# Mixer projection begins with index and latent columns; its other four groups become units beside preparing, turning and index; modulation spread 13, 13, 10 over three stages

## The reference

```python
(q_a, k_a, v_a, f_a, q_b, k_b, v_b, q_c, c_kv, q_i, k_i, w_i, gates) = jnp.split(h @ w_in, _split_points(), axis=-1)
y_a = forgetting_attention(heads(q_a, 6), heads(k_a, 6), heads(v_a, 6), f_a + b_forget)   # cumulated log sigmoid(f) as bias
y_b = stick_breaking_attention(heads(q_b, 5), heads(k_b, 5), heads(v_b, 5))
k_c, v_c = jnp.split(rmsnorm(c_kv, g_kv) @ w_kv_up, 2, axis=-1)
q_c, k_c, q_i = partial_rope of each;  k_i = partial_rope(rmsnorm(k_i, g_idx_k))
y_c = dsa_attention(q_c, k_c, v_c, q_i, k_i, w_i)   # keys: the top 64 of an index score relu(q_i k_i) w_i
merged = g_a*(y_a @ w_up_fox) + g_b*(y_b @ w_up_sb) + g_c*(y_c @ w_up_dsa);  return merged @ w_out
```

## Time and profile before

| | us |
|---|---|
| Median of 3 runs (2890.78 to 2898.58) | 2893.74 |
| The profiled execution | 2897.77 |
| Its span, first to last instruction | 2896.0 |
| PE busy | 2670.3 (92%) |
| DVE busy | 1427.1 (49%) |
| ACT busy | 1188.7 (41%) |
| Mean granted TensorE clock, as share of full | 0.946 |

### The profile page before, as it was taken

How to read it: one execution, slowest core, us unless ns; L and a number is a source line. 1 busy time by engine, 2 the same in 40 slices (tenths; PEclk the granted TensorE clock), 3 DMA queues, 4 the chain that set the end, 5 groups by cost and what they waited for, 6 DMA issues and landing times.

```text
span 2896.0 us, 32848 instructions
## 1 busy us (share of the span) xinstructions
PE 2670.3 (92%) x12253; PEld 2119.9 (73%) x12253; DVE 1427.1 (49%) x1731; ACT 1188.7 (41%) x1356; POOL 91.6 (3%) x73
## 2 busy tenths in 40 slices
PE   7999788899999979789989989987999999998998
PEld 6878446678788754567878878876677878876786
DVE  4554543655554544365455455444235455455544
ACT  4445126344444431544444444444124444454433
POOL 0000011000000010200000000020000000000000
PEclk9999999999999999899999999999569999998999
DMA  6555792455555559445554545545014545544453
GB/s 209 189 167 179 260 321 84 144 180 187 167 184 187 179 198 339 143 135 191 188 165 160 188 144 190 188 129 180 1 44 160 186 148 190 188 165 136 157 188 115
DMA packets 329761, 496.08 MB, mean 171 GB/s; under 512 B 13326, under 2 KB 218410, under 8 KB 329546
## 3 DMA queue, kind: packets, MB, share of 16 engines
q1 hardware_dynamic: 327322, 487.98, 51.0%
q0 software_dynamic: 2064, 5.84, 1.1%
q10 hardware_dynamic: 288, 1.05, 0.1%
HBM read 493.77 MB, written 1.05 MB: 171 GB/s over the span
## 4 chain that ended last, share of the span: by engine, by line
PE 86%; DVE 5%; ACT 3%; DMA 3%; issue 1%; DVEq 0%; ACTq 0%; POOL 0%; SPq 0%; PEldq 0%
PE ps L660 80%; PE ps L744 2%; PE ps L863 2%; DVE wlo L407 1%; ACT whi L392 1%; DMA raw<-in_mod_w_dram 1%; DMA raw<-in_w_in_dram 1%; PE ps L751 1%; DMA raw<-in_even_w_in_dram 1%; PE ps L677 1%; PE ps L699 0%; PE ps L834 0%; ACT arena L1091 0%; DVE arena L1426 0%; ACT L1265 0%
## 5 line engine op out<-in xcount | busy, mean ns | idle before, releaser
L407 DVE TENSOR_TENSOR wlo<-raw,whi 128x2048 fp32r<-128x2048 f32 (+5 forms) x405 | 883.6, 2183 | 686.0 <-ACT whi L392 667.7
L660 PE MATMUL ps<-whi,HThi 128*128 128x512 f32 (+1 forms) x2360 | 947.1, 401 | 71.9 <-ACT arena L1091 23.5
L392 ACT ACTIVATE whi<-raw 128x2048 fp32r<-128x2048 f32 (+4 forms) x405 | 752.7, 1860 | 464.3 <-PE ps L660 410.5
L660 PE MATMUL ps<-wlo,HThi 128*128 128x512 f32 (+1 forms) x2360 | 930.2, 394 | 0.0
L660 PE MATMUL ps<-whi,HTlo 128*128 128x512 f32 (+1 forms) x2360 | 929.7, 394 | 0.0
L660 PEld LDWEIGHTS ps<-whi,HThi 128*128 128x128 f32 x2360 | 452.0, 192 | 174.8 <-issue 26.1
L660 PEld LDWEIGHTS ps<-wlo,HThi 128*128 128x128 f32 x2360 | 451.1, 191 | 96.4
L660 PEld LDWEIGHTS ps<-whi,HTlo 128*128 128x128 f32 x2360 | 452.4, 192 | 89.0
L660 PE MATMUL ps<-whi,AThi 128*128 128x512 f32 x792 | 310.0, 391 | 1.1
L660 PE MATMUL ps<-wlo,AThi 128*128 128x512 f32 x792 | 308.5, 390 | 0.0
L660 PE MATMUL ps<-whi,ATlo 128*128 128x512 f32 x792 | 308.2, 389 | 0.0
(11 more groups left out here) (190 smaller groups left out, 1652.3 us busy)
## 6 DMA issues: line engine op xcount, KB each, us to landing
raw<-in_ffn_w_dram SPq DMA_DIRECT2D x330, 512.0 KB, 4.1
raw<-in_w_ffn_gu_dram SPq DMA_DIRECT2D x176, 512.0 KB, 4.6
raw<-in_mod_w_dram SPq DMA_DIRECT2D x72, 1024.0 KB, 7.0
raw<-in_w_ffn_down_dram SPq DMA_DIRECT2D x88, 512.0 KB, 4.1
raw<-in_w_in_dram SPq DMA_DIRECT2D x44, 1024.0 KB, 5.1
raw<-in_even_w_in_dram SPq DMA_DIRECT2D x12, 1024.0 KB, 5.1
raw<-in_conv_w_in_dram SPq DMA_DIRECT2D x12, 1024.0 KB, 5.1
raw<-in_w_out_dram SPq DMA_DIRECT2D x8, 1024.0 KB, 5.0
```

The source lines that it names most:

```text
L392: i = nc.scalar.activation(whi[0:rows, r, a:b], raw[0:rows, r, a:b], ACT.Copy)
L407: i = nc.vector.tensor_tensor(wlo[0:rows, r, a:b], raw[0:rows, r, a:b], whi[0:rows, r, a:b].bitcast(F32), ALU.subtract)
L660: return nc.tensor.matmul(o, lhsT, rhs, start=first, stop=last)
```

## The change

The dense phase of each first-block mixer has two groups only: columns 2438 to 2890 (latent, index, w_i: 452) and 1926 to 2438 (512). The projection's other four groups (three of 512 columns, one of 390) are units beside, letter J; their result is evicted by ACT with a copy instead of a sigmoid. Chunks to transpose are in two parts: those that index needs (7, phase turn_index) come before index, the other 12 (turn_rest) behind it, and the forget sum moves from prepare and latent to turn_rest. Each mixer now has 13 groups of modulation beside it (46 steps in all), and 10 groups (20 units) go beside neighbourhood attention, one unit per step; the last layer's scale gains are therefore computed in a later phase. The pace is a table instead of constants.

```diff
-BESIDE = "GmmmGmmmmmmmmmmmmmmmGGGG"
+PJ_FIRST = ((CKV, NPJ), (1926, CKV))
+PJ_LATER = ((1414, 1926), (902, 1414), (390, 902), (0, 390))
+BESIDE = ("JmJJmJmGmmmmmGmmmmmGGGG", "JmJJmJmGmmmmmGmmmmmGGGG", "mmmmmmmmmm")
+PACE = (dict(prepare=2, latent=2, heads=2, index=(1, 1, 1, 1), rest=(2, 2), item=(1,) * 11 + (0,), stick=1),
...
+        dict(item=(1, 1)))
...
-            for n0 in range(0, NPJ, 512):
-                n = min(512, NPJ - n0)
-                gs.append(wide_group(w, n0, n, ("copy", [PJ[:, b, n0:n0 + n] for b in range(NB)])))
-            phase("dense", groups=gs, rstd=rstd, after_norm=True, conditions=l == 0)
...
+            phase("dense", groups=[projected(*ends) for ends in PJ_FIRST], rstd=rstd, after_norm=True, conditions=l == 0)
...
+                elif what == "J":
+                    us, n, ev = projected(*next(later), rstd)
...
+                if what != "m" and n == 512:
                     pool_units.extend(u for u, _ in us)
...
-            for kind in ("prepare", "latent", "turn_heads", "index", "softmax", "stick"):
+            phase("beside", steps=steps, pace=PACE[l])
+            for kind in ("prepare", "latent", "turn_index", "index", "turn_rest", "softmax", "stick"):
...
                 phase("near_turn")
+                steps = []
+                for _ in BESIDE[2]:
+                    us, n, ev = mod_group()
+                    steps += [("unit", us, j, ev) for j in range(2)]
+                phase("beside", steps=steps, pace=PACE[2])
                 phase("near")
+                phase("beside_end")
...
-        AT_PREPARE, AT_LATENT, AT_HEADS, AT_INDEX, AT_ITEM, AT_STICK = 4, 2, 3, 4, 1, 1
...
+                elif kind == "turn_index":
+                    turn(index_chunks(), "heads_turned", ("heads_read_dve", "heads_read_act"))
+                    beside.go(beside.pace["heads"])
+                elif kind == "turn_rest":
+                    turn(rest_chunks(), "heads_turned", ("heads_read_dve", "heads_read_act"))
+                    beside.go(beside.pace["rest"][0])
+                    take("forget_log")
+                    mm(ps[:, 4, 0:HF], cc("upto"), fl2[:, 0, :])
...
+                    beside.go(beside.pace["rest"][1])
+                    take("forget_copied")
...
+                    w, f = ev[1][0].shape[-1], ACT.Sigmoid if ev[0] == "sigmoid" else ACT.Copy
                     for b in range(NB):
-                        i = A(ev[1][b], ps[:, 6 + b, :], ACT.Sigmoid, scale=ev[2][:, b:b + 1])
+                        i = A(ev[1][b], ps[:, 6 + b, 0:w], f, scale=ev[2][:, b:b + 1])
```

More of the change, by code:

```diff
@@ L206, in vcols, with mod_group @@
             return vec[:, r:r + DC]
+        mod_groups = iter([(l, r) for l in range(DEPTH) for r in range(NMOD * D // 512)])
+        def mod_group():
+            l, r = next(mod_groups)
+            group = wide_group(t["mod_w_2"][l], r * 512, 512, ("mod", l, r * 512 // P))
+            whole_units.update(u for u, _ in group[0])
+            return group
         for l in range(DEPTH):
@@ L350, in copy_turned @@
                             rows = blocks[0].shape[-1]
-                            i = copy(TT[0:rows, m + j, :], ps[0:rows, (m // 2) % 4, j * SEQ:(j + 1) * SEQ])
+                            i = copy(TT[0:rows, first + m + j, :], ps[0:rows, (m // 2) % 4, j * SEQ:(j + 1) * SEQ])
                         i.then_inc(sem(read), 1)
@@ L419, in upto, with begin, index, item @@
                     self.at += 1
-        AT_PREPARE, AT_LATENT, AT_HEADS, AT_INDEX, AT_ITEM, AT_STICK = 4, 2, 3, 4, 1, 1
         class Beside:
             def __init__(self, step):
-                self.step, self.steps, self.at = step, [], 0
-            def begin(self, steps):
-                self.steps, self.at = steps, 0
+                self.step, self.steps, self.at, self.pace = step, [], 0, {}
+            def begin(self, steps, pace):
+                self.steps, self.at, self.pace = steps, 0, pace
+            def index(self, *quarters):
+                self.go(sum(self.pace["index"][q] for q in quarters))
+            def item(self, n):
+                self.go(self.pace["item"][n % len(self.pace["item"])])
             def go(self, n=None):
@@ L619, in _ @@
                         u = us[j][0]
-                        if u in whole_units:
+                        if u not in pool_units:
                             continue
@@ L666, in three, with turn @@
                 return mm(o, lh, wl, False, last)
-            def turn(chunks, done, freed, first=0):
+            def turn(chunks, done, freed):
                 for m, blocks in enumerate(chunks):
@@ L951, in _ @@
                 elif kind == "beside":
-                    beside.begin(ph["steps"])
+                    beside.begin(ph["steps"], ph["pace"])
                 elif kind == "beside_end":
@@ L1079, in exps @@
                       accum_out=rsum[:, n:n + 1]).then_inc(sem("item_exp"), 1)
-                    beside.go(AT_ITEM)
-                beside.go(2 * AT_ITEM)
+                    beside.item(n)
+                for n in (len(items), len(items) + 1):
+                    beside.item(n)
                 take("item_turned", min(2, len(items)))
@@ L1471, in _ @@
                     if ph.get("gains"):
-                        for l in range(DEPTH):
+                        for l in ph["gains"]:
                             for s3 in range(3):
```

132 lines of the change are left out of this document (71 added, 61 removed).

## The result

The changed kernel takes 2949.4 us (median of 4 runs, 2947.8 to 2951.1) against 2896.2 (4 runs): ratio 1.0177, 95% interval 1.0155 to 1.0198, slower by 53. Its profiled execution has a span of 2946.6, 50.6 more than before.

The account below looks back on a forecast made before the run. PE, busy 92% of the span, was taken as the bound through its work, waits and clock. Mixers 0, neighbourhood attention +5, barriers +1 made +6 on the profiled 2897.8; against the median, 4.0 lower, 2900, range 2862 to 2954.

Parts of the forecast that it names:

- the clock stays at 1.2 GHz in neighbourhood attention: Rival: neighbourhood attention stays at half clock throughout, +41 there and +11 behind it, 2948 us; chance 0.30.
- Work moved in the front, 17 us: Mixer's front: one gate group (10.9) and 5 of 13 modulation units (6) leave, 17 us shorter if waits stayed.
- The three new waits, 5.5, 10 and 6.3: PE idle at latent's end 5.5 us, in index ahead of the last J group 10, at index's end 6.3.
- The low clock behind them: Mixer's front: after the wait in index the clock is low, costing 2.5 us more.
- Softmax and stick, +1: Softmax and stick of each mixer: 19.9 us go out and 20.6 come in, so +1.
- Each mixer even, 12 us of error for both: Both mixers: front -1 and softmax with stick +1 give 0, with 12 us of error on either side.
- Neighbourhood attention, rise after four items, -6, and +11 behind: Neighbourhood attention: clock rises after about four items, 105 us, -6; output projection's late loads behind it +11; +5 together.
- full clock from nearly the first item: Rival: neighbourhood attention runs at full clock almost from its start, -13 in all, 2881 us; chance 0.17.
- rival of short waits: Rival: waits in the mixers' fronts are shorter than laid out, -30, neighbourhood as forecast, 2867 us; chance 0.15.

Follow-up runs that it names:

- 2932.0: Changed kernel with the gate group in the middle of softmax moved behind all modulation; measured 2932.0 us, ratio 1.0123.
- reordered projection groups: Changed kernel with last projection group ahead of second modulation group, middle gate group behind all modulation, neighbourhood units in first 14 steps; 2910.7 us, ratio 1.0049.
- old mixers: Kernel before with modulation spread 13, 13, 10, softmax units in its first 14 steps, all 20 neighbourhood units within the first 14 steps; 2846.9 us, ratio 0.9832.
- 2855.2: Kernel before with modulation spread 13, 13, 10 and softmax's 14 units in its first 14 steps instead of over 24; 2855.2 us, ratio 0.9861.
- 2854.6: Kernel before with 17 modulation groups per mixer and only four units beside neighbourhood attention, in its first four items; 2854.6 us, ratio 0.9851.

## Why the prediction came out as it did

The forecast was 2900 and no change; measured is 2949.4, inside the range, and slower. The time is that of the rival "the clock stays at 1.2 GHz in neighbourhood attention", and its mechanism did not happen: that stage got faster. So the number 2948 was met for the wrong reason. By the steps:

- *Work moved in the front, 17 us.* Right: 109.9 to 92.9.
- *The three new waits, 5.5, 10 and 6.3.* Right in place and cause, 5.6, 8.0 and 6.6. Idle time rose by 14.9.
- *The low clock behind them.* I counted 2.5 us, behind one of them. Lost time rose by 6.2. With this the front came out at +4.2 for -1.
- *Softmax and stick, +1.* This step failed: 157.7 became 179.4, +21.7, the same in both mixers. Its work term was right: 10.9 in, 6.4 out, +4.5 expected, 4.4 measured. The rest was not. I let 10.4 us of waits go with the units that had made them and put 9.7 back; idle time rose by 6.4. And I let 3.1 us of low clock go, with nothing put back; lost time rose by 11.0. That is 14.1 of the 20.7 us that this step is off. Where half of it was is shown: 6.8 of lost time hung on the gate group in the middle of softmax (2932.0 for 2949.4).
- *Each mixer even, 12 us of error for both.* Idle time I had at +12.8 and work at -12.5, measured +21.2 and -12.9; lost time I had at -0.6, measured +19.4. The clock, in each stage, is the larger part of the error.
- *Neighbourhood attention, rise after four items, -6, and +11 behind.* The rise came at the end of the first unit (0.55 up to 2099.4, then 1.00): the rival "full clock from nearly the first item", -13, measured -11.8. Steps took 5.19 and 4.73, on average 4.96 where I had priced 5.27; the pause at the end took 8.8 for 8. The rule of the Trainium skill that transposes don't count (TensorE: Matmul & The Clock Gate, Part 4) I had held to be against this trace; the rise here has a modulation unit in it and no transposes of rows yet, so it doesn't bear the rule out or contradict it.
- *The chances.* Slower had the largest share, 0.46, but for the wrong case. The case that came, mixers losing through the clock, had none of its own: I had tied the clock to neighbourhood attention alone and treated it as nearly constant in the mixers. The rival of short waits was also summed wrongly, without effect here: its -30 with the +6 of the rest is 2870, not 2867.

Still open: why the first mixer's softmax had 0.83 and the second's 0.95 with the same order and the same wait ahead of it; whether the place of the units or the kind of the items beside them decides in softmax; and the 29 us a mixer between the reordered projection groups and the old mixers: 19 are idle time, 11 of them in the front, and 11 lost time; it was not taken apart further.

## What to carry to other kernels

Sum a schedule in three columns, work, idle and lost to the clock; a plan that is right in the first two can be wrong by the third, which follows each pause. Filler work beside a thin stage can be worth more than its own time. In the two stages measured here it was best placed at the stage's start (2855.2 and 2854.6 for 2896): there it kept or lifted the clock, and at the end it would have delayed what comes next. Try the order and read the clock of both mixers; it is no fixed rule, since behind a pause at softmax's start the clock came back after 5.7 us in one mixer and only after 27.6 in the other, with a unit in each step of both. Keep unsplit quick units away from the front of units that must be loaded and split: the wait moves to whoever is queued behind.

## What the runs showed of the hardware

- The same steps can run at either clock, with PE busy in both, by what ran ahead of them. Neighbourhood attention's items stood at 0.50 through 110.9 busy us, and at 1.00 for 53.1 us behind four modulation units.
- Not every kind of step keeps a full clock. Forgetting items alone lost it after 2.5 us (349.7) and stood at half clock until 394.1; index items kept it without a unit from 399.9 to 416.1, behind a gate unit.
- The clock's rise is not tied to the instructions alone: with the same instructions behind the same 17.88 us wait it came 27.6 us behind softmax's start in one mixer and 5.7 in the other.
- A busy PE is no sign of a full clock: 46.4 of 47.2 us busy at 0.57. In neighbourhood attention PE was busy 98% of the stage at 0.50 and 96% in the run with four units, which was 43 us shorter: a stage that loses to the clock looks better used.
- Ten units more or less beside softmax made no difference of time (88.8 and 88.1 us), while 14 units in another order made 18.
